# Hybrid decoder block: two of the three gate products of the merge as a 2x2x2 block product with seven block multiplications

## The reference

```python
p = h @ w_in                      # holds, among others, gate_logits (3 x 1024 columns)
y_a, y_b, y_c = ...               # widths 256, 256, 512
g_a, g_b, g_c = jnp.split(jax.nn.sigmoid(gate_logits), 3, axis=-1)
merged = g_a * (y_a @ w_br_a) + g_b * (y_b @ w_br_b) + g_c * (y_c @ w_br_c)
x1 = x + gt1 * (merged @ w_out)   # then router and 32 experts
```

## Time and profile before

| | |
|---|---|
| median of 3 runs | 1779.69 us (1779.67 to 1782.38) |
| span of the profiled execution | 1778.4 us (no separate run time is listed for it; the span is 1.3 us under the median) |
| TensorE, VectorE, ScalarE, GpSimd busy | 94%, 57%, 25%, 12% of the span |
| time mix stage, first scores to the merge's A part | about 575 to 1023 us |
| one chunk of it | 55.8 us |

### The profile page before, as it was taken

The page is one execution under the profiler, slowest core; times in us unless marked ns, Lnnn a source line. Parts: engine busy times, 40 slices in busy tenths (PEclk is TensorE's granted clock), DMA queues, the critical chain, the costliest instruction groups (busy, mean ns, idle before and its releaser), DMA issues.

```text
span 1778.4 us, 35422 instructions
## 1 busy us (share of the span) xinstructions
PE 1670.4 (94%) x14793; PEld 930.9 (52%) x14793; DVE 1012.6 (57%) x2453; ACT 442.4 (25%) x1072; POOL 211.8 (12%) x311
## 2 busy tenths in 40 slices
PE   5999999999999999999999999987999999999990
PEld 3455444544444545555455545545777775555550
DVE  2486526555555354443544435555778877776754
ACT  5120324333444212222122121112222122122110
POOL 3030000000110222202222051010000000000003
PEclk9999999999999999999999999988999999999995
DMA  9377218001211110101101176489899999999997
GB/s 350 120 265 252 71 71 263 25 24 32 63 48 52 47 33 16 33 21 31 34 16 33 56 292 232 148 284 370 330 425 427 426 427 426 429 427 427 429 422 303
DMA packets 109014, 363.70 MB, mean 205 GB/s; under 512 B 12890, under 2 KB 56840, under 8 KB 96428
## 3 DMA queue, kind: packets, MB, share of 16 engines
q1 hardware_dynamic: 86256, 282.70, 41.0%
q10 hardware_dynamic: 15708, 54.73, 8.4%
q0 software_dynamic: 6960, 25.04, 3.8%
HBM read 316.42 MB, written 58.74 MB: 211 GB/s over the span
## 4 chain that ended last, share of the span: by engine, by line
PE 80%; DMA 14%; DVE 3%; POOL 1%; issue 1%; ACT 1%; SPq 1%; ACTq 0%; POOLq 0%; DVEq 0%
PE bank L298 78%; DMA arena<-in_w_e_out 11%; DMA arena<-in_w_in 1%; POOL arena L759 1%; PE bank L945 1%; DMA arena<-y_slots,ints 1%; SPq L380 1%; DVE arena L2396 0%; DVE arena L1887 0%; PE bank L1233 0%; ACTq L1397 0%; DMA arena<-in_kn_g_c 0%; DVE arena L2386 0%; ACT arena L1523 0%; DMA x_slots<-arena,ints 0%
## 5 line engine op out<-in xcount | busy, mean ns | idle before, releaser
L298 PE MATMUL bank<-arena 128*32 128x256 f32 (+7 forms) x14414 | 1627.4, 388 | 36.4 <-DMA arena<-in_w_e_in 7.1
L298 PEld LDWEIGHTS bank<-arena 128*32 128x32 f32 (+3 forms) x14414 | 884.7, 131 | 748.5 <-issue 548.1
L2386 DVE STREAM_TRANSPOSE arena<-arena 32x256 f32<-32x256 f32 x372 | 161.9, 435 | 5.7
L2396 DVE STREAM_TRANSPOSE arena<-arena 32x128 f32<-32x128 f32 x384 | 157.5, 410 | 4.8
L1725 ACT ACTIVATE arena<-bank 128x128 f32<-128x128 f32 x96 | 19.7, 278 | 395.4 <-PE bank L298 395.4
L1717 ACT ACTIVATE arena<-arena 128x96 f32<-128x96 f32 x248 | 92.1, 460 | 5.2 <-DVE arena L2386 5.2
L2377 DVE TENSOR_TENSOR arena<-bank,arena 128x512 f32<-128x512 f32 x64 | 35.5, 557 | 99.9 <-PE bank L298 99.8
L2144 DVE TENSOR_TENSOR arena<-arena,bank 128x128 f32<-128x128 f32 (+1 forms) x40 | 11.4, 286 | 130.3 <-PE bank L298 130.3
L759 POOL DMA_INDIRECT arena<-y_slots,ints x16 | 17.1, 1070 | 542.9 <-DMA y_slots<-arena 537.9
L684 POOL TENSOR_TENSOR arena<-arena 64x256 f32<-64x256 f32 x96 | 70.2, 731 | 30.3 <-DVE arena L2120 23.7
L1887 DVE RECIPROCAL arena<-arena 128x512 f32<-128x512 f32 x10 | 33.5, 3349 | 30.8 <-ACT arena L1452 30.8
(11 more groups left out here) (337 smaller groups left out, 1030.1 us busy)
## 6 DMA issues: line engine op xcount, KB each, us to landing
arena<-in_w_e_in SPq DMA_DIRECT2D x64, 2048.0 KB, 24.4
arena<-in_w_e_out SPq DMA_DIRECT2D x32, 2048.0 KB, 25.2
arena<-in_w_ada SPq DMA_DIRECT2D x12, 2048.0 KB, 12.4
arena<-in_w_in SPq DMA_DIRECT2D x32, 512.0 KB, 3.8
arena<-x_slots ACTq DMA_DIRECT2D x32, 512.0 KB, 10.3
y_slots<-arena ACTq DMA_DIRECT2D x32, 288.0 KB, 9.3
y_slots<-arena POOLq DMA_DIRECT2D x21, 384.0 KB, 17.2
arena<-in_w_in SPq DMA_DIRECT2D x3, 2048.0 KB, 21.3
```

The source lines that it names most:

```text
L298: return nc.tensor.matmul(o, l, r, start=start, stop=stop)
L2386: ins = V.transpose(e_xT[s][ts(b, QT), :, ts(t, QT)], rows[:, :, b, :])
L2396: ins = V.transpose(hT[ts(q, QT), :, ts(t, QT)], e_h[ts(c, QT), r, :].rearrange("p (n k) -> p k n", k=4))
```

## The change

Gates B and C for 128 output channels and 512 tokens are one product of a 2 x 2 block matrix of weights (rows: gate C, gate B; columns: the two halves of the 1024 input channels) with a 2 x 2 block matrix of `HT` (rows: the halves of the input channels; columns: two quarters of 256 tokens). It is computed with seven block multiplications (the Winograd form). There are 16 such units u, two for each chunk of `tmix`; a unit has 7 x 4 matmuls of 256 columns. Then:

- The four sums of token blocks, `T1` to `T4`, are made once for each half of the tokens by GpSimd during `mlstm(c)` and stored to a new DRAM tensor `token_blocks`, as are the three plain blocks by SP. Seven blocks of 512 KB then lie over `HT` and are loaded once before unit 0 and again in unit 7.
- GpSimd makes four sums of weight blocks for each unit (`weight_sums`) and most of the sums of the seven products (`gate_sums`); VectorE makes two (`product_sums`); ScalarE copies the products out of banks 6 and 7 (`product_out`).
- The branch matmuls of unit u (4 + 2, still 512 columns) run after the gate matmuls of unit u + 1. The last six run after `tmix(7)`.
- `side` has 40 slots for a chunk in place of 44, each of one 512-column or two 256-column matmuls.
- The sigmoid is one operation of 128 x 1024 for each unit; VectorE's `gated` has the same four products of 128 x 512 for each chunk, two in steps q = 2 and 3, and two directly behind `operands(c + 1)`.
- In memory the merged rows lie in another order; `w_br_a` is loaded at the end of the stage, and two expert loads wait for `o_mm` 10 and 14 in place of 4 and 12.

```diff
+            def gate_product(u, p, k):
+                bank, o = ((6, 0), (6, 256), (7, 0), (7, 256), (6, 0), (6, 256), (7, 256))[p]
+                if k == 0:
+                    if p in (0, 2, 4, 6):
+                        pe.wait_ge(sem(f"tb{p // 2}_in"), at(f"tb{p // 2}_in") + 16 * (1 + u // KT))
...
+                w = FW[:, 4 * p + k, :] if p < 2 else FWB[:, 4 + k, :] if p == 2 else W_SUM[p - 3][:, k, :]
+                ins = mm(PS[bank][:, o:o + 256], w, TB[p][:, k, :], k == 0, k == 3)
...
+            def branch(u, k):
...
+                if k == 0 and u < NU - 1:
+                    pe.wait_ge(sem("g_sum"), at("g_sum") + u + 2)
...
-                side(c, first, 36, 44)
+                side(c, 36, 40)
                 if c < NT - 1:
                     scores(c + 1)
...
+            for k in range(6):
+                branch(NU - 1, k)
             y_turned(NT - 1)
...
+            def weight_sums(u):
+                pool.wait_ge(sem("raw_in"), at("raw_in") + 32 * u + 32)
...
+                G.tensor_tensor(W_SUM[0], a21, a22, ALU.add).then_inc(sem("s_made"), 1)
+                pool.wait_ge(sem("s_made"), at("s_made") + 4 * u + 1)
+                G.tensor_tensor(W_SUM[1], W_SUM[0], a11, ALU.subtract).then_inc(sem("s_made"), 1)
+                G.tensor_tensor(W_SUM[2], a11, a21, ALU.subtract).then_inc(sem("s_made"), 1)
+                pool.wait_ge(sem("s_made"), at("s_made") + 4 * u + 3)
+                G.tensor_tensor(W_SUM[3], a12, W_SUM[1], ALU.subtract).then_inc(sem("s_made"), 1)
...
+                if c:
+                    merge(2 * c - 2)
+                gate_sums(2 * c)
+                weight_sums(2 * c + 1)
+                if c:
+                    merge(2 * c - 1)
+                gate_sums(2 * c + 1)
+                if c < NT - 1:
+                    weight_sums(2 * c + 2)
...
+            raw_weights(0)
+            sp.wait_ge(sem("tb_st"), at("tb_st") + 16 * 6)
+            sp.wait_ge(sem("tf_st"), at("tf_st") + 128)
+            for g in range(4):
+                token_blocks(0, g)
```

More of the change, by code:

```diff
@@ L234, in hybrid_block, with merged @@
         GA = [HT[:, c] for c in range(KT)]
-        MP = [PA[:, 2 + t] for t in range(6)] + [KK[:, 0], KK[:, 1]]
+        def merged(t, k):
+            row, c = 2 * (t % 4) + k % 2, 4 * (t // 4) + k // 2
+            return PA[:, 2 + row, ts(c, P)] if row < 6 else KK[:, row - 6, ts(c, P)]
         YT = [PA[:, 0], PA[:, 1], QK[:, 0], QK[:, 1], QC[:, 0], QC[:, 1], QC[:, 2], QC[:, 3]]
@@ L1059, in _ @@
                     front(c + 1)
[L1060 to L1081, removed]
-                        pe.wait_ge(sem("mix_done"), NT + NT)
[L1083 to L1089, removed]
@@ L1091, in scores, with side @@
+            def side(c, j0, j1):
+                for j in range(2 * j0, 2 * j1):
+                    u, r = 2 * c + j // 40, j % 40
+                    if r < 28:
+                        gate_product(u, r // 4, r % 4)
+                    elif u and r % 2 == 0:
+                        branch(u - 1, (r - 28) // 2)
             def scores(c):
@@ L1114, in tmix @@
             def tmix(c, first=False):
-                side(c, first, 0, 4)
+                side(c, 0, 4)
                 if c:
@@ L1170, in tmix @@
                 ins.then_inc(sem("a_WU"), 1)
-                side(c, first, 32, 34)
+                side(c, 32, 34)
                 pe.wait_ge(sem("a_WUs"), c + 1)
@@ L1183, in tmix @@
                 ins.then_inc(sem("a_GS"), 1)
-                side(c, first, 34, 36)
+                side(c, 34, 36)
                 pe.wait_ge(sem("a_Qs"), c + 1)
@@ L2160, in tmix @@
                         ins.then_inc(sem("a_Tt"), 1)
-                    if q in (1, 4):
-                        gated(c, q // 4, first)
+                    if q == 1:
+                        product_sums(2 * c)
+                    if q == 6:
+                        product_sums(2 * c + 1)
                     if q == 2 and c < NT - 1:
                         middles(c + 1)
-                gated(c, 2, first)
+                    if q in (2, 3) and c:
+                        gated_half(2 * c - 1, q - 2, (mp, m_t)[q - 2], 4 + q)
                 dve.wait_ge(sem("a_GS"), c + 1)
```

290 lines of the change are left out of this document (216 added, 74 removed).

## The result

The change makes the kernel slightly slower: 1787.03 us median of 17 runs (1784.31 to 1791.28) against 1782.49 us of the kernel before on the same chips (17 runs), a ratio of 1.0028 with an interval of 1.002 to 1.0036. That is +5 us where the forecast was -9. In the two profiled executions the span went from 1778.4 to 1785.0 us, +6.6.

The account below looks back on a forecast made before the run. The prediction took TensorE's own work to bound the stage, with VectorE bounding the border after the change. Its terms, -14.7 + 2.1 + 3.4 - 3.4 + 0.8 + 2.7 = -9.1 us, took 1779.7 to 1770.6, range 1763 to 1784.

Parts of the forecast that it names:

- TensorE's work: Each chunk's source matmuls: 37.75 us falls to 34.32, 3.43 less, with 256-column records at 0.2145 us.
- rival 2: Pace of 256-column records on TensorE: at 0.25 us each the gain is gone, 1787.6 us; chance 0.05.
- The border: From `a_Y` to the next chunk's first `a_A1`: VectorE's chain limits the gain to 2.10 us, seven times, -14.7.
- Rival 1: GpSimd's weight sums collide with VectorE at borders: one collision each 1779.5 us, chance 0.15; two 1788, chance 0.08.
- the margin to the *operands: At each border, GpSimd's sums end at 737.1, 0.8 us before VectorE's first operand operation at 737.90.
- rival 1 with two collisions: Two GpSimd and VectorE collisions at each of seven borders, needing GpSimd 2 us late: +17.8, 1788 us; chance 0.08.
- The wait in q = 2: First branch matmul of each chunk but the first waits 0.3 us for both `product_sums`, seven times: +2.1.
- Chunk 0: Start of the stage: +3.4 idle for token blocks, -3.4 for missing filler, +0.8 for a lowered clock.
- The missing filler: Chunk 0, q = 2 and 3: no earlier branch, 5.15 us of filler missing, -3.4 net.
- The end: Chunk 7: normalization starts 2.05 us later and `gated(15)` adds 0.62, +2.7; six branch matmuls lie within it.
- Work at no cost: Token sums in mLSTM chunks, block stores beside attention and GpSimd's 30 us a chunk were to cost nothing.
- the clock term of the start: Clock lost after TensorE's idle start in chunk 0: +0.8 us, half of a window's 1.7, with 0 and 1.7 kept.

Follow-up runs that it names:

- experiment 2: Changed kernel with VectorE's `bonus_keys` moved from just ahead of `a_Y` into step q = 4 of the next chunk: 1785.37 us, ratio 1.001 to the kernel before.
- Experiment 3: Changed kernel with SP's six plain-block stores issued inside the column-load loop and no token sums in mLSTM chunk 5: 1786.16 us, ratio 1.002 to the kernel before.
- experiment 6: Kernel before the change, with only GpSimd's level blocks held back until VectorE's first `a_Tt`: 1782.98 us, ratio 0.9995 to the kernel before.
- five small edits: Changed kernel with needless start-stall matmuls, `bonus_keys` moved, stores and token sums moved, end weights and `gated` moved, level blocks held back: 1775.57 us, ratio 0.9949.
- experiment 5: Changed kernel with GpSimd's level blocks `a_lo(1)` to `a_lo(5)` held back until VectorE's first `a_Tt`: 1785.02 us, ratio 1.0005 to the kernel before.
- experiment 7: Changed kernel with level blocks held back, first token blocks loaded ahead of gate B's weights, first weight sums behind the fourth level block: 1780.53 us, ratio 0.9985.
- experiment 1: Changed kernel with four needless 512-column matmuls on TensorE during the start stall, results unread: 1786.42 us, ratio 1.0012 to the kernel before.

## Why the prediction was wrong, step by step

**TensorE's work.** The pace of 256 columns was right: in an undisturbed run (24 records, 5.34 us, the last one 0.38) they start (5.34 - 0.38) / 23 = 0.216 apart, 0.2145 predicted, so rival 2 is out.

```profile
753.25 5.34 PE L326 MATMUL bank<-arena 128*128 128x256 f32 x24
```

Yet a chunk's busy time fell by 2.92 and not 3.43. 112 records at 0.0015 more make 0.2, which is a real loss. Most of the other 0.3 is the count: ahead of a wait a record is busy to its own end (0.59 us for 512 columns, 0.38 for 256), where in a run the next one starts before that, 0.16 at the scores and 0.06 at `a_A1`. So these two waits delay TensorE by 0.87 and 0.97, not by 0.71 and 0.90.

**The border.** VectorE's chain is its bound, as predicted, and from where VectorE takes up `a_Y` to the first `a_A1` the step is 2.1 us shorter, as predicted. But VectorE takes it up 0.7 late, and on TensorE the step is only 1.49 shorter (19.02 to 17.53) where the forecast had 2.10: the scores wait 0.7 (0.25 predicted), `a_A1` 0.9 (1.08 predicted). Rival 1 had the collision of weight sums and VectorE, and it put its price at the wrong place. I measured the margin to the *operands* and found 0.8 us. The sums never reached them: the last ended at 742.78, 0.6 behind `a_Y`, about where the forecast had it, and lines 2188 to 2191 ran at 0.42. They hit lines 2364 and 2182, ahead of `a_Y`. Rival 1 even counted these "three two-operand operations of VectorE that take turns with them", but only what they cost GpSimd, since they stood in VectorE's idle time: 0.42 + 0.61 became 1.48 + 2.70, and cover of 2.44 was less than the 3.15 added. The difference is 0.7 late, the wait that experiment 2 took away, and then the border was the forecast's. Of the 0.8 us that an inner chunk gained less than forecast, 0.6 are this and 0.2 the pace. The time of rival 1 with two collisions, 1788, and that of rival 2, 1787.6, lie beside the measured 1787.0 by luck: a border lost 0.6 and not 2.5 us to collisions, and the pace was not 0.25. The rule of the Trainium skill ("SBUF — State Buffer", section "SBUF: two separate sides") of an exclusive lock for the full instruction agrees with every one of these rows, line 2319's 1.52 against 0.59 the cleanest.

**The wait in q = 2** was 0.3, seven times, as predicted.

**Chunk 0** was to lose 0.8 and then gain at its border, -2.4 in all; it is +1.7. The stall was 3.7 (3.4 predicted). The clock behind it was mis-sized: 2.9 and not 0.8. I had halved what a window with a quarter of idleness had lost, where of the 16 records behind a stall of 3.7 us all but the last two started 0.43 us apart, at half rate; 0.57 granted over the window 586 to 593. The Trainium skill ("TensorE: Matmul & The Clock Gate", Part 1) has an idle array gated down to half its rate; the trace agrees, and I should have priced the records behind the stall, not a share of a window. Another 0.6 went to ScalarE's copy (line 1725) of the last mLSTM result out of bank 7, which product 2 needs; the forecast had no such term. The missing filler was as forecast: steps q = 1 to 3 took 10.5 us in place of 13.8. Counted as delay of TensorE, with the 0.6 of the scores and the 0.2 of pace, that makes 0.4 + 2.1 + 0.7 + 0.6 + 0.2 = 4.0 of the 4.1 us between forecast and trace.

**The end.** +2.7 with the waits of chunk 7 made 4.1, and 5.2 were measured: 1.5 of it ahead of the last `a_Y` (1.4 forecast) and 3.7 behind (2.7 forecast). The mechanism was right as far as it went. Normalization starts 4.23 us behind VectorE's taking up `a_Y`, 2.18 before, the 2.05 of the forecast. What was mis-sized is the rest of the chain: lines 2382 and 2383 took 0.80 and 0.63 us where they take 0.17 and 0.43 in the other chunks, beside GpSimd's `merge` (lines 794 and 795), which makes 0.8. And the forecast missed a second bound of the same length. TensorE had 5.15 us of branch matmuls left behind the 3.43 of filler, and stood 1.7 for their weights, which can't be loaded until branch 14 has let go of the buffer. I had let the six matmuls "lie in" VectorE's chain and not seen the wait for the single buffer; they held the turned `y` and ended 0.1 us later than VectorE could have used them. No experiment took away one of the two bounds alone.

**Work at no cost.** Two of its items cost. The stores of the plain blocks do run beside attention, but SP stood at the sixth for 35 us and with it the third column load: 1.0 us. The token sums collide as well: in mLSTM chunk 5, whose root lies on a chain that TensorE waits for, VectorE's line 2129 took 2.49 in place of 0.43 beside one, and 1.1 us came out (a gap of 0.8). Experiment 3 took both back. GpSimd's "30 us a chunk fit in 55.8" was true (28.80) and beside the point.

**What stays open.** The remaining 2.1 of the +4.2 ahead of the stage, and the 1.5 in the experts' stage. The first is made of 0.8 in the first loads and 1.3 of low clock behind a wait at 261 that both kernels have: from 261 to 264 the clock granted is 0.50 in the changed kernel and in experiment 6's profile of the kernel before, and 1.00 in the kernel before and in experiment 3. The second is in waits for loads, and that stage's length goes from 755.4 to 758.6 over the ten profiles, with the same code there. No experiment was aimed at either, so I count them neither for nor against the change. The single profiles differ by 6.6 and the medians by 4.5.

So the failed step is the one that took the work in VectorE's and the queue's idle time as free and put the only margin at the operands, together with the clock term of the start. The six inner chunks gained 6.0 us and not 10.8, mostly because VectorE was 0.7 late at each `a_Y`. The other rows of the ledger cost 12.6 and not 1.7: 4.2 ahead of the stage (0 forecast; 2.1 of it stores and token sums), 4.1 more in chunk 0 (2.1 of it the clock), 1.1 more at the end, and 1.5 behind it that stay open.

## What to carry to other kernels

When work is given to GpSimd, list every VectorE instruction that works on SBUF alone and could fall beside it, not only those on the critical path: a VectorE that has 2.4 us of idle time loses it to three GpSimd additions. Price single events one by one (a stall with the records behind it at half clock, a buffer that can't be refilled, a DMA queue that is full), since a saving of 1 us in each of seven chunks is smaller than four of them. And before giving up on such a change, look at what is in reach: five small edits, none of which touches the products, turned +5 into -9 us.

## What the runs showed of the hardware

- After 3.7 us of idleness 16 matmuls of 256 columns took 6.60 us in the changed kernel and 5.28 in experiment 5; after 2.11 us of it (experiment 7), and with TensorE kept busy (experiment 1), 3.72. The same stall does not always cost the same.
- A later wait shows the same. Behind 1.9 us for the last branch weights the clock granted in experiment 1 fell to 0.66, behind the 1.7 of the changed kernel it stayed at 1.00:

```profile
1020.00:1025.00 5.00, 4.62 (x7) 2.03 (x8) 4.34 (x11) 2.55 (x3) 0.77 (x2) 0.66 0.93 342
```
```profile
1022.00:1027.00 5.00, 5.00 (x14) 2.16 (x12) 4.35 (x12) 2.55 (x3) 0.01 (x1) 1.00 0.98 397
```

- Issuing three stores of 512 KB took SP 2.35 us in experiment 3. Of six in the changed kernel, issued while the DMA engines were busy with loads, five took 4.80 us and the sixth 35.4 (DMA share 1.05 and 360 GB/s meanwhile).
- Beside a GpSimd TENSOR_TENSOR these VectorE operations on SBUF alone stretched: 128x256 from 0.42 to 1.48 us, 128x260 from 0.43 to 2.49, two of 64x128 from 0.59 to 1.52, and a TENSOR_SCALAR of 128x4 from 0.17 to 0.80.
